# Plain alternation of wide and narrow products, and new places of the low weight parts

## The reference

```python
        h = rms_norm(x, ln_pre_g[layer])
        proj = jnp.einsum('bsd,de->bse', h, w_in[layer])
...
        y_rnn = jnp.einsum('bsc,cd->bsd', hr * jax.nn.silu(rnn_gate), w_rnn_out[layer])
...
        y = jnp.einsum('bsd,de->bse', merged, w_o[layer])
        x = x + rms_norm(y, ln_post_g[layer])
...
    u = h @ w_in
...
    y = gates[:, :, 0] * (branches[0] @ w_branch[0])
    for n in range(1, N_BRANCH):
        y = y + gates[:, :, n] * (branches[n] @ w_branch[n])
    return y @ w_out
```

## Time and profile before

| | |
|---|---|
| median of two runs | 3122.79 us |
| the profiled execution | 3123.54 us |
| its span, first to last instruction | 3121.6 us |
| granted TensorE clock | 0.998 |
| PE busy, share of the span | 3100.0 us, 99% |
| DVE busy | 2129.6 us, 68% |
| ACT busy | 1734.3 us, 56% |
| L544 wide matmuls (5728 on hT, 1664 on uT, 896 token-major) | 8288 |
| matmul instructions in all | 18230 |

### The profile page before, as it was taken

The page is one execution under the profiler, slowest core; times in us unless marked ns, Lnnn a source line. Parts: engine busy times, 40 slices in busy tenths (PEclk is TensorE's granted clock), DMA queues, the critical chain, the costliest instruction groups (busy, mean ns, idle before and its releaser), DMA issues.

```text
span 3121.6 us, 52176 instructions
## 1 busy us (share of the span) xinstructions
PE 3100.0 (99%) x18230; PEld 2732.4 (88%) x18230; DVE 2129.6 (68%) x2741; ACT 1734.3 (56%) x2291; POOL 0.2 (0%) x4
## 2 busy tenths in 40 slices
PE   8999999999999899999999999999999999999999
PEld 7888888888888789888888888888888888888888
DVE  7677575766667687766766656777776676665675
ACT  5685444444445556656565555645665656555563
POOL 0000000000000000000000000000000000000000
PEclk9999999999999999999999999999999999999999
DMA  7656665555556565565556666566556555665555
GB/s 230 197 171 202 200 190 169 187 180 172 179 174 211 174 176 159 158 203 173 177 172 194 189 182 182 183 205 185 159 158 203 173 177 172 194 189 183 181 183 180
DMA packets 569809, 571.67 MB, mean 183 GB/s; under 512 B 26352, under 2 KB 565488, under 8 KB 569712
## 3 DMA queue, kind: packets, MB, share of 16 engines
q1 hardware_dynamic: 569712, 570.42, 59.3%
HBM read 568.25 MB, written 2.10 MB: 183 GB/s over the span
## 4 chain that ended last, share of the span: by engine, by line
PE 98%; DVE 1%; ACT 1%; issue 0%; DMA 0%; SPq 0%; ACTq 0%; DVEq 0%
PE pg L544 92%; PE pa L783 1%; PE pa L800 1%; PE pa L544 1%; PE pa L790 1%; PE pa L759 1%; PE pa L801 1%; PE pa L716 0%; DVE hl L1288 0%; PE pa L890 0%; DMA raw<-w_in 0%; ACT hl L945 0%; DVE uT L1369 0%; DVE xres L1747 0%; PE pa L739 0%
## 5 line engine op out<-in xcount | busy, mean ns | idle before, releaser
L544 PE MATMUL pg<-hT,hl 128*128 128x512 f32 x11456 | 2003.8, 335 | 0.9 <-DVE hl L1288 0.9
L544 PEld LDWEIGHTS pg<-hT,hl 128*128 128x128 f32 x11456 | 1742.6, 188 | 241.8 <-DVE hl L1288 4.6
L1288 DVE TENSOR_TENSOR hl<-raw,hl 128x1024 fp32r<-128x1024 f32 (+1 forms) x1071 | 1255.6, 1209 | 304.5 <-ACT hl L945 296.2
L945 ACT ACTIVATE hl<-raw 128x1024 fp32r<-128x1024 f32 (+1 forms) x1071 | 1085.4, 1044 | 300.9 <-PE pg L544 278.9
L544 PE MATMUL pg<-uT,hl 128*128 128x256 f32 (+1 forms) x3712 | 631.4, 331 | 16.9 <-DVE uT L1369 7.9
L544 PEld LDWEIGHTS pg<-uT,hl 128*128 128x128 f32 x3712 | 555.7, 189 | 88.4 <-issue 14.8
L953 ACT ACTIVATE corr<-pg 128x512 f32<-128x512 f32 x286 | 170.3, 595 | 820.8 <-PE pg L544 820.8
L544 PE MATMUL pg<-hl,hT 128*128 128x256 f32 (+1 forms) x1792 | 318.7, 337 | 0.0
L544 PEld LDWEIGHTS pg<-hl,hT 128*128 128x128 f32 x1792 | 276.3, 188 | 39.7
L1295 DVE TENSOR_TENSOR work<-pg,corr 128x512 f32<-128x512 f32 (+1 forms) x154 | 105.8, 687 | 294.5 <-ACT corr L953 294.0
L1120 ACT ACTIVATE work<-work,sm 128x256 f32<-128x256 f32 (+3 forms) x144 | 69.3, 482 | 130.3 <-DVE sm L1566 128.3
(11 more groups left out here) (191 smaller groups left out, 1369.3 us busy)
## 6 DMA issues: line engine op xcount, KB each, us to landing
raw<-w_in SPq DMA_DIRECT2D x791, 512.0 KB, 4.7
raw<-w_br SPq DMA_DIRECT2D x96, 512.0 KB, 4.5
raw<-w_out SPq DMA_DIRECT2D x64, 512.0 KB, 4.7
raw<-w_rnn SPq DMA_DIRECT2D x32, 512.0 KB, 4.7
raw<-w_o SPq DMA_DIRECT2D x32, 512.0 KB, 5.2
raw<-w_att SPq DMA_DIRECT2D x16, 512.0 KB, 4.3
raw<-w_uq SPq DMA_DIRECT2D x16, 384.0 KB, 4.0
tab<-tabs SPq DMA_DIRECT2D x5, 896.0 KB, 7.0
```

Source lines behind the costliest of these rows:

```text
L544: return nc.tensor.matmul(out, lhsT, rhs, start=start, stop=stop, skip_group_check=True)
L945: nc.scalar.activation(part(j, 0, h, 0, n), raw[:, bass.ds(j % 2 * UC + a, n)], ACT.Copy)\
L1288: tt(part(j, 1, h, 0, n), raw[:, bass.ds(j % 2 * UC + a, n)], part(j, 0, h, 0, n).bitcast(F32), ALU.subtract).then_inc(lo_done, 1)
```

## The change

1. The tables and sets `ends`, `RUNS`, `ALL`, `AGAIN` and `SIDE` go, and with them every `side` and `sides` argument. `in_order` now always alternates wide and narrow.
2. The low part of each half moves by its own step, `LO_MORE`: 16 and 48 numbers in the halves of the first slot, 64 and 96 in those of the second, which is 64, 192, 256 and 384 bytes. From 256 bytes beyond the activations modulo 512 they come to 320, 448, 0 and 128. The high parts stay at 192.
3. `HL` grows by 256 numbers (1024 bytes), so `hT` and `uT` keep their place modulo 512.
4. `both_view` takes the new distance between high and low parts, so the two parts of a streamed token-major operand lie by other distances too.

```diff
-SIDE = {
-    "RX": {4: AGAIN},
...
-    "1": {15: ends(0, 2), 16: ends(1, 0), 17: ends(0, 1), 18: ALL, 19: ends(1, 0), 20: ends(0, 1), 21: ends(1, 1),
...
-HI_AT, LO_AT, SLOT, HL = 16, UC + 32, 2 * UC + 128, 4 * UC + 224
+HI_AT, LO_AT, SLOT, HL = 16, UC + 32, 2 * UC + 128, 4 * UC + 480
+LO_MORE = ((16, 48), (64, 96))
...
-            first = j % 2 * SLOT + (LO_AT if e else HI_AT) + h * UC // 2 + a
+            first = j % 2 * SLOT + (LO_AT + LO_MORE[j % 2][h] if e else HI_AT) + h * UC // 2 + a
...
-            def in_order(ks, subs, side, wide, narrow):
-
-                if RUNS in side and len(ks) == 4 and ks[0] % 8 == 0:
-                    for k in ks:
-                        for s in range(subs):
-                            wide(k, s)
-                    for k in ks:
-                        for s in range(subs):
-                            ins = narrow(k, s)
-                    return ins
+            def in_order(ks, subs, wide, narrow):
+
                 for k in ks:
                     for s in range(subs):
                         wide(k, s)
-                        if k % 8 not in side:
-                            ins = narrow(k, s)
-                    if k % 8 in side:
-                        for s in range(subs):
-                            ins = narrow(k, s)
+                        ins = narrow(k, s)
                 return ins
...
-                    pair = hl[:, first:first + 2 * (LO_AT - HI_AT)].rearrange("p (e n) -> p e n", e=2)
+                    pair = hl[:, first:first + 2 * (LO_AT + LO_MORE[j % 2][h] - HI_AT)].rearrange("p (e n) -> p e n", e=2)
...
-            product(U_WO, C_WO, h3, lambda q: pe.wait_ge(mix_ready, 1 + q), by_bank=True,
-                    sides=((), AGAIN))
+            product(U_WO, C_WO, h3, lambda q: pe.wait_ge(mix_ready, 1 + q), by_bank=True)
```

More of the change, by code:

```diff
@@ L90 @@
 }
[L94 to L100, removed]
-SIDE = {
-    "RX": {4: AGAIN},
-    "RG": {3: ends(0, 1), 4: ends(1, 0), 7: ends(0, 1), 8: ends(1, 0), 11: ends(0, 1), 12: ends(1, 0), 15: ends(0, 1),
-           16: ends(1, 0), 21: ends(0, 1), 22: AGAIN, 23: ends(0, 1), 24: AGAIN},
-    "1": {15: ends(0, 2), 16: ends(1, 0), 17: ends(0, 1), 18: ALL, 19: ends(1, 0), 20: ends(0, 1), 21: ends(1, 1),
[L108 to L114, removed]
 MAPS = {"1": 3, "A": 1, "B": 2, "C": 1}
@@ L562, in in_order, with feature_major @@
                         wide(k, s)
-                        if k % 8 not in side:
-                            ins = narrow(k, s)
-                    if k % 8 in side:
-                        for s in range(subs):
-                            ins = narrow(k, s)
+                        ins = narrow(k, s)
                 return ins
-            def feature_major(b, subs, wh, wl, op, ks, start, stop, base, side):
+            def feature_major(b, subs, wh, wl, op, ks, start, stop, base):
                 return in_order(
-                    ks, subs, side,
+                    ks, subs,
                     lambda k, s: mm(pg3[:, b + s, :], wh[k - base][:, s * P:s * P + P], op[:, k, :], start and k == ks[0], False),
@@ L576, in feature_major, with token_major @@
                                     stop and k == ks[-1]))
-            def token_major(b, hiw, both, op, ks, start, stop, base, side):
+            def token_major(b, hiw, both, op, ks, start, stop, base):
                 return in_order(
-                    ks, 2, side,
+                    ks, 2,
                     lambda k, s: mm(pg3[:, b + s, :], op[:, k, s * P:s * P + P], both[k - base], start and k == ks[0], False),
@@ L614, in opening @@
                             ins = feature_major(2 * h, 2, wh, wl, u3, ks, q == 0 and n == 0, q == 3 and n == len(parts) - 1,
-                                                4 * q - 4 * h, ALL)
+                                                4 * q - 4 * h)
                         ins.then_inc(half_done, 1)
@@ L618, in opening, with unit @@
                             summed()
-            def unit(u, j, c, cj, op, first, last, form="f", subs=2, ready=None, halves=(0, 1), first_parts=None, side=()):
+            def unit(u, j, c, cj, op, first, last, form="f", subs=2, ready=None, halves=(0, 1), first_parts=None):
                 base = 0 if first else 8
@@ L640, in unit, with product @@
                         if form == "r":
-                            ins = feature_major(b, subs, wh[h], wl[h], op, ks, begin, end, base + 4 * h, side)
+                            ins = feature_major(b, subs, wh[h], wl[h], op, ks, begin, end, base + 4 * h)
                         elif form == "t":
-                            ins = token_major(b, wh, both_view(j, CH), op, ks, begin, end, base, side)
+                            ins = token_major(b, wh, both_view(j, CH), op, ks, begin, end, base)
                         else:
-                            ins = feature_major(b, subs, wh, wl, op, ks, begin, end, base, side)
+                            ins = feature_major(b, subs, wh, wl, op, ks, begin, end, base)
                     ins.then_inc(half_done, 1)
-            def product(u0, c0, op, ready, by_bank=False, sides=((), ())):
+            def product(u0, c0, op, ready, by_bank=False):
                 chunks = NCH // 2 - by_bank
@@ L654, in product @@
                             unit(u0 + 4 * i + 2 * j + k, k, c0 + 2 * i + j, j, op, k == 0, k == 1,
-                                 ready=(lambda ks: ready(ks[0] // 4)) if j == 0 else None,
-                                 side=sides[j] if k == 0 else ())
+                                 ready=(lambda ks: ready(ks[0] // 4)) if j == 0 else None)
                 if by_bank:
@@ L679, in h_split, with half_product @@
                 return lambda q: pe.wait_ge(h_ready, 4 * n + q + 1)
-            def half_product(u0, c0, count, sides=((), ())):
+            def half_product(u0, c0, count):
                 with pe.Fori(0, NCH // 2) as i:
@@ L685, in half_product @@
                         unit(u0 + 2 * i + j, j, c0 + 2 * i + j, j, u3, True, True, form="k",
-                             ready=lambda ks: pe.wait_ge(u_ready, count - 7 + ks[-1]), side=sides[j])
+                             ready=lambda ks: pe.wait_ge(u_ready, count - 7 + ks[-1]))
             def post_sum():
@@ L727, in _ @@
                     unit(U_RX + 2 * c + j, j, C_RX + c, c, u3 if c < RAW_CHUNKS else h3, j == 0, j == 1,
-                         ready=(lambda ks: h_split(0)(ks[0] // 4)) if c == RAW_CHUNKS else None,
-                         side=SIDE["RX"].get(2 * c + j, ()))
+                         ready=(lambda ks: h_split(0)(ks[0] // 4)) if c == RAW_CHUNKS else None)
             for c in range(2 * NCH):
                 for j in range(2):
-                    unit(U_RG + 2 * c + j, j, C_RG + c, c, h3, j == 0, j == 1, side=SIDE["RG"].get(2 * c + j, ()))
+                    unit(U_RG + 2 * c + j, j, C_RG + c, c, h3, j == 0, j == 1)
                 for _, q in rec_pe[c]:
@@ L857, in pair @@
                                 pe.wait_ge(evac_done, c + (2 if n == 1 else 5))
-                            unit(u + n, n, None, at // 2, h3, n in (1, 4), n in (3, 5), halves=halves, side=ALL)
+                            unit(u + n, n, None, at // 2, h3, n in (1, 4), n in (3, 5), halves=halves)
                     elif what in "uh":
@@ L862, in pair @@
                         is_v = (kind == "1" and 6 <= cc < 9) or (kind in "BC" and cc == 2)
-                        unit(u + n, n, c + cc, cc, h3, n % 2 == 0, n % 2 == 1, "t" if is_v else "f", halves=halves,
-                             side=SIDE[kind].get(n, ()))
+                        unit(u + n, n, c + cc, cc, h3, n % 2 == 0, n % 2 == 1, "t" if is_v else "f", halves=halves)
                     elif what == "norm":
@@ L913, in _ @@
                                  (lambda ks: h_split(1 + l)(ks[0] // 4)) if c == RAW_HEAD else None, halves=halves,
-                                 first_parts=FIRST_TILES[0:3] if (l, c, j) == (0, 0, 0) else None,
-                                 side=SIDE["head"][l].get(2 * c + j, ()))
+                                 first_parts=FIRST_TILES[0:3] if (l, c, j) == (0, 0, 0) else None)
                             if (c, j, halves[0]) == ((1, 0, 1), (0, 1, 0))[l]:
@@ L926, in _ @@
                             pair(kind, l, p, ul + LU[kind] + p * units(kind), cl_ + LC[kind] + p * CHUNKS[kind], 2 * n)
-                    half_product(ul + LU_BR[kind], cl_ + LC_BR[kind], 2 * (PAIRS + 12 * l + 4 * PI[kind] + PAIRS),
-                                 {"A": (ends(4, 0), ()), "B": ((), ()), "C": (ALL, AGAIN)}[kind])
+                    half_product(ul + LU_BR[kind], cl_ + LC_BR[kind], 2 * (PAIRS + 12 * l + 4 * PI[kind] + PAIRS))
                 product(ul + LU_WO, cl_ + LC_WO, h3, lambda q: pe.wait_ge(mix_ready, 4 * l + 5 + q),
```

## The result

The forecast was 3157 us, in a range from 3100 to 3205. The changed kernel takes 3169.51 us (two runs, 3169.12 and 3169.89) against 3122.79 us: 1.0149 times the time of before, with a 95% interval of 1.013 to 1.0168. It is slower, by less than 2%. The profiled execution has a span of 3167.2 us, 45.6 us longer than before.

What follows compares the result with a forecast made beforehand. The prediction took PE, busy 99% of the span, as the bound, through the distances between fp32r matmul starts. From 3122.8 us, minus 17 for the order, plus 52 for the low parts, it forecast 3157 us, range 3100 to 3205.

Steps and rivals of the forecast that it cites:

- I take 7 for all four: Low parts at their four new places: 7 ns more a pair, over 7392 pairs 52 us; bounds 0 and 14 ns.
- the row of token-major: Nearest measured case for place 320: matmuls of 392 and 279 ns against 389 and 276, 6 ns a pair.
- the sums of squares: Nearest measured case for place 0: 64 matmuls with stream and weights from `uT`, 394 ns, 5 over the cheap wide one.
- the upper bound: Most a new low-part place was expected to cost: 14 ns a pair, a little over the dearest state read, 11.
- The saving of 17 us: Plain alternation: 15.8 us from 1760 rearranged pairs at 9 ns, 1.4 us from dear stretches, if all were cheap.
- Whatever state one half settles in, the next must find anew: Low parts: second reason for a cost above zero, as the place changes with every half-unit, every 2.7 us.
- Token-major, taken at nothing within 4.5 us: 896 token-major pairs: only the second half of a wide stream moves; no cost taken, 5 ns either way being 4.5 us.
- A: Rival for the matmul pairs: new places free alternation from dear states, every half at 340 ns, 3106 us; chance 0.2.
- B: Rival: places do nothing; each return from work on `pa` draws a cheap or dear state; 3143 to 3180 us; chance 0.2.
- C: Rival: load meets stream in one spot throughout, 354 ns a pair or over in most halves, 3209 us; chance 0.17.
- D: Rival: 14 ns of a cheap pair is collision the right place removes; 2990 us, or 3050 with two places; chance 0.05.
- The loop at 510 to 558 us: Sign in the profile after: product stretches, all at 340 ns a pair before, must become dearer if place matters.

Runs made afterwards that it cites:

- places-only run: Kernel before with the low parts moved to 320, 448, 0 and 128 and its order tables kept: 3172.78 us, 1.0161 times before.
- order-only run: Changed kernel with the old places (all low parts at 256), so plain alternation alone against the kernel before: 3129.97 us, 1.0023 times before.
- 320 everywhere: Changed kernel with all four low parts at 320 bytes beyond the activations modulo 512, plain alternation kept: 3164.53 us, 1.0134 times before.
- 448 everywhere: Changed kernel with all four low parts at 448 bytes beyond the activations modulo 512, plain alternation kept: 3195.68 us, 1.0233 times before.

## Why the prediction was right, and where its steps were off

*What bounds the kernel.* Right. PE's waits and the splits did not move, and all of the 46 us is in the distances between matmuls.

*The direction and the mechanism.* Right: the new places of the low parts make the pairs dearer. The places-only run shows that they cost all of the change.

*The two terms of the sum.* The order was to save 17 us and cost 7 (order-only run), an error of 24 us. The low parts were to cost 52 us; the step from the order-only kernel to the changed one is 39.5 us, 5.3 ns for each of the 7392 pairs, an error of 12 us the other way. So the net of 47 us against 35 is as near as it is in part by luck.

*"I take 7 for all four".* The term was meant as a distance from a kernel that holds 340 everywhere, 3106 us. No run is such a kernel. From 3106 to 3169.5 us it is 63.5 us, 8.6 ns a pair, and the medians of the four places, 349.8 on average, lie 9.8 ns over 340: by this measure 7 was too small. For 320 the row of token-major was a good neighbour, 6 expected and 6.9 measured, though the place has a second level at 353. For 0 the sums of squares were not, 5 expected and 9.8 measured; they are wide matmuls behind wide ones, not alternation. 448, without a row, costs 14, the upper bound, and 128, without one too, 8.5.

*The saving of 17 us.* As a saving from the order it failed. Alone, plain alternation costs 7 us, since behind work on `pa` it takes the dear level in about a quarter of the halves and holds it. The prediction counted rearranged pairs as a cost of 9 ns and did not price what they avoid, though it had read both levels at one place. Its own condition, "if the cheap state held everywhere", did not hold.

*"Whatever state one half settles in, the next must find anew".* The runs show no cost of this, rather the opposite: with 320 everywhere 29% of the halves were dear and the dear level was held for whole stretches, with changing places 16% at that place were.

*Token-major, taken at nothing within 4.5 us.* Right: its 112 halves took 312.1 us before and 313.4 after, by the starts in the two traces.

*The rivals.* A fell: no usual place but 192/256 is at 340 in most halves. B, that only the state counts, fell as a whole with the kernel with 448 everywhere, and is right as a part: several places have two or three levels, and which one a half takes is not settled by its place. What settles it was not tested by itself. C is what 448 everywhere does. D, the floor under 340, found nothing.

The Trainium skill, "SBUF — State Buffer", section "Who interferes with whom", says that "PE and ACT never wait on anyone". Taken as the prediction took it, that TensorE's two operands don't disturb each other, it does not fit these runs: places alone moved the kernel by 2.1%, between 3129.97 and 3195.68 us.

*What the profile would show.* 396 ns for the wide matmul on `hT`, as written for this case, though 395 was written for B and the two can hardly be told apart. The loop at 510 to 558 us became dearer, as written, and this sign is the one that speaks against B. Each half has its own distance, as written; that at 448, 354 ns, lies outside the 340 to 350 given.

## What to carry to other kernels

In this kernel, which a stream of fp32r matmuls bounds, the price of a pair depends on where the loaded weights lie relative to the streamed activations, modulo 512 bytes, for both kinds of matmul together. In a kernel of this kind, try places before orders: here they moved the time by 66 us, and the order by 7. Read the price from the length of a long steady stretch by its number of matmuls. The mean durations in a short stretch point to it, but not sharply: their sum was 675 at the 353 level of place 320, and 679 in the half at 448, which is at 354. A steady distance can have two levels at one place, and the level is held until something disturbs it, so look at the same loop at two times in the trace before giving it one price. When the layout changes, measure the order anew, and do so stretch by stretch.

## What the runs showed of the hardware

In runs of at least six alternating halves at one distance, a wide and a narrow matmul take 340.0 and 350.0 ns in the order-only kernel, 346.7 and 353.3 with 320 everywhere, and 353.3 and 348.9 with 448 everywhere. So the distances are few and sharp, and all but the last are multiples of 3.33 ns. A held level outlasts a great deal: in the order-only kernel the dear one goes on from 2003 us through 656 matmuls. The same kernel differs from run to run by 7 us (3125.83 to 3132.55 in ten runs), more than the kernel before does on the same chip (3121.44 to 3124.93 in 13). That other halves take the dear level in other runs would explain it, but one run alone was traced. Why the cheap pair is cheap, and whether it is the load and the stream themselves that collide, these runs do not tell; the splits beside them are made unlikely by the 347.1 ns with and without them.
